# Feed-forward stages of 768 tokens: gate and up as seven quarter products, down in six groups

## What is computed

```python
D_MODEL, SEQ, CTX_LEN, DEPTH, D_FF = 1024, 512, 256, 2, 2816
def swiglu(h, w_gu, w_down):
    gate, up = jnp.split(h @ w_gu, 2, axis=-1)
    return (jax.nn.silu(gate) * up) @ w_down
for l in range(DEPTH):
    h = h + 0.5 * m[2] * swiglu(modulate(rms_norm(h, norm_ffn1[l]), m[0], m[1]), ffn1_w_gu[l], ffn1_w_down[l])
    ...   # the same for the context tokens, then the projection in, four mixers, the projection out
    h = h + 0.5 * m[8] * swiglu(modulate(rms_norm(h, norm_ffn2[l]), m[6], m[7]), ffn2_w_gu[l], ffn2_w_down[l])
```

## Time and profile before

| | |
|---|---|
| median of 3 runs | 3365.09 us (3362.91 to 3369.96) |
| the profiled execution's own time | 3367.02 us |
| its span | 3365.3 us |
| mean granted clock of TensorE | 0.985 |
| PE matmul busy | 3231.2 us, 96% |
| PE weight load busy | 2765.1 us, 82% |
| DVE busy | 1817.0 us, 54% |
| ACT busy | 1157.8 us, 34% |
| POOL busy | 439.7 us, 13% |

### The profile page before, as it was taken

One profiled execution on the slowest core, in us unless ns is written; L12 is line 12 of the kernel. 1 busy time (PEld: TensorE's weight loads), 2 busy tenths in 40 slices (PEclk: granted clock), 3 DMA queues, 4 the chain that ended last, 5 costly groups with the idle time before them and its releaser, 6 DMA issues. The chain is left out here.

```text
span 3365.3 us, 67083 instructions
## 1 busy us (share of the span) xinstructions
PE 3231.2 (96%) x28066; PEld 2765.1 (82%) x28066; DVE 1817.0 (54%) x2677; ACT 1157.8 (34%) x1839; POOL 439.7 (13%) x312
## 2 busy tenths in 40 slices
PE   6999999999988999999999999999999989899998
PEld 5888888886667878888888888888886668789897
DVE  4552554565667655543554553454555766655353
ACT  3331222225665333321222431222224654344231
POOL 2000001000705310000002000001100616120000
PEclk9999999999999999999999999999999999999999
DMA  5231221342000012222221222222232000122222
GB/s 201 91 109 66 94 96 60 127 156 89 1 17 3 4 57 81 93 98 77 90 90 57 94 98 71 81 93 85 85 141 110 2 18 3 34 88 94 90 91 94
DMA packets 68270, 263.34 MB, mean 78 GB/s; under 512 B 7552, under 2 KB 8704, under 8 KB 67456
## 3 DMA queue, kind: packets, MB, share of 16 engines
q1 hardware_dynamic: 67664, 256.95, 22.1%
q10 hardware_dynamic: 432, 3.88, 0.3%
HBM read 258.70 MB, written 2.10 MB: 77 GB/s over the span
## 5 line engine op out<-in xcount | busy, mean ns | idle before, releaser
L240 PE MATMUL ps<-hn_hi,w_hi 128*128 128x512 f32 (+1 forms) x3520 | 864.8, 327 | 17.9 <-DVE hn_lo L457 5.9
L240 PE MATMUL ps<-hn_hi,w_lo 128*128 128x512 f32 (+1 forms) x3520 | 865.4, 327 | 0.0
L240 PE MATMUL ps<-hn_lo,w_hi 128*128 128x512 f32 (+1 forms) x3520 | 861.1, 326 | 0.0
L217 ACT ACTIVATE w_hi<-raw 128x1024 fp32r<-128x1024 f32 (+1 forms) x300 | 338.5, 1128 | 1375.4 <-PE ps L240 1217.7
L222 DVE TENSOR_TENSOR w_lo<-raw,w_hi 128x1024 fp32r<-128x1024 f32 (+1 forms) x300 | 396.9, 1323 | 469.5 <-ACT w_hi L217 462.0
L240 PEld LDWEIGHTS ps<-hn_hi,w_hi 128*128 128x128 f32 x3520 | 547.9, 190 | 82.3 <-issue 17.6
L240 PEld LDWEIGHTS ps<-hn_lo,w_hi 128*128 128x128 f32 x3520 | 548.3, 190 | 58.3
L240 PEld LDWEIGHTS ps<-hn_hi,w_lo 128*128 128x128 f32 x3520 | 545.2, 190 | 58.1
L240 PE MATMUL ps<-g_hi,w_hi 128*128 128x512 f32 (+1 forms) x1424 | 398.0, 347 | 6.1 <-DVE g_lo L894 6.1
L240 PE MATMUL ps<-g_lo,w_hi 128*128 128x512 f32 (+1 forms) x1424 | 403.5, 351 | 0.0
L240 PE MATMUL ps<-g_hi,w_lo 128*128 128x512 f32 (+1 forms) x1424 | 397.5, 347 | 0.0
(11 more groups left out here) (274 smaller groups left out, 3795.8 us busy)
## 6 DMA issues: line engine op xcount, KB each, us to landing
raw<-wgu SPq DMA_DIRECT2D x176, 512.0 KB, 3.4
w_mod_one<-wmod SPq DMA_DIRECT2D x100, 512.0 KB, 3.3
raw<-wdn SPq DMA_DIRECT2D x64, 704.0 KB, 4.1
raw<-win SPq DMA_DIRECT2D x44, 512.0 KB, 4.5
w_mod_two<-wmod SPq DMA_DIRECT2D x28, 512.0 KB, 3.6
w_mod_first<-wmod_first SPq DMA_DIRECT2D x4, 2048.0 KB, 23.2
raw<-wout SPq DMA_DIRECT2D x16, 512.0 KB, 3.3
h<-xT ACTq DMA_DIRECT2D x1, 3072.0 KB, 9.8
```

The source lines that it names most:

```text
L217: act.activation(w_hi[s][:, 0:kt, :].rearrange("p k n -> p (k n)"), raw[s][:, 0:kt * P], ACT.Copy).then_inc(hi_ready[s].sem, 1)
L240: mm = pe.matmul(out[:, o:o + b - a], w[:, k, :], m[:, k, a:b], start=(k == 0 and w is w_hi[s] and m is mov_hi), stop=(k == kt - 1 and w i ...
```

## The change

For the three stages of 768 tokens `ffn` is replaced by `ffn_seven`; the last stage keeps `ffn`. The hidden tiles are taken in six groups of 4, 2, 4, 4, 4 and 4. The first group (4 pairs) is made as before, 96 matmuls to a pair. While it runs, DVE and ACT make the moving operands of the others: the normed tokens (`x_norm`) in quarters, by half of the contraction and half of the tokens, four sums of quarters, and the high and low parts of seven moving operands of 4 tiles by 386 columns.

Each of the other 18 pairs is a 2 by 2 block product (gate and up by the two halves of the contraction, times the two halves of the contraction by the two halves of the tokens) made with seven products of quarters. A quarter product has 4 contraction tiles, three products each, one span of 386 columns: 12 matmuls, 84 to a pair. DVE makes four sums of weight quarters (`weight_sum`) and the low parts; the seven results go to seven of the eight PSUM banks in turn and are put together by one ACT copy and seven DVE additions. Each weight slot has one buffer.

After each group come 8 down products over its 4 (or 2) hidden tiles, 24 (or 12) matmuls each; in the first two of them (four, in the group of 2) the last contraction tile is put off. DVE adds each to `h`, so 48 additions in a stage where there were 16. The modulation vectors stay 24 in number: two in each pair of the first group, one in pair 7, and five in the down part of each of the groups j = 2, 3 and 4. The loops are written out. The stride of `hn_hi` and `hn_lo` goes from 784 to 772 columns, and buffers are moved; the down weights are laid out in HBM in loads of 512 KB.

The diff, cut to what sets the order on each engine:

```diff
-NTP = 784
+NTP = 772
+DOWN_SIZES = (4, 2, 4, 4, 4, 4)
+            mods_of = {n: (2 * n, 2 * n + 1) for n in range(PLAIN)}
+            mods_of[FIRST[2] + 1] = (8,)
+            mods_of.update({("down", j): tuple(range(5 * j - 1, 5 * j + 4)) for j in (2, 3, 4)})
...
+            def weight_sum(eng, p, n):
+                a, b, op = {2: (quarter(2), quarter(3), ALU.add), 3: (slot_sum[2][:, :], quarter(0), ALU.subtract),
+                            4: (quarter(0), quarter(2), ALU.subtract), 5: (quarter(1), slot_sum[3][:, :], ALU.subtract)}[p]
+                slot_free(eng, p, n)
...
+                eng.tensor_tensor(slot_sum[p][:, :], a, b, op).then_inc(w_summed.sem, 1)
...
+                def _(sp):                     # loads, after a group of four pairs
+                        if z == 4:
+                            lo_there(sp, j, "01")
+                            load(0, DOWN[j, 2])
+                            lo_there(sp, j, "2")
+                            lo_there(sp, j, "3")
+                            load(1, DOWN[j, 3])
...
+                        for m in mods[:1]:
+                            load_mod(m)
+                        for s, src in enumerate(srcs):
+                            for unit in freed_by[s]:
+                                lo_there(sp, j, unit)
+                            load(s, src)
+                            for m in mods[1:] if s == 0 else ():
+                                load_mod(m)
...
+                def _(act):                    # one pair of the 18
+                            first_copy(n)
+                            if not last_of(n):
+                                gate_hi_made(n + 1)
...
+                            gate_out(n, 0)
+                            if not last_of(n):
+                                for p in (2, 3, 4):
+                                    slot_hi_made(p, n + 1)
...
+                            gate_out(n, 1)
+                            if not last_of(n):
+                                slot_hi_made(6, n + 1)
+                                slot_hi_made(5, n + 1)
+                            ring_hi_made(n, 0)
+                            ring_hi_made(n, 1)
...
+                def _(dve):
+                    def way_down(j):
...
+                        for unit in ("3", "4", "5") if z == 4 else ():
+                            down_lo_made(dve, j, unit)
...
+                        for m in mods[:1]:
+                            mod_product(m)
+                        for t in range(KD):
+                            if j < LAST and t == 7:
+                                (slot_lo_made if z == 4 else weight_sum)(dve, 5 if z == 4 else 4, n)
+                            add_down(j, t)
...
+                            if z == 4 and t == 1:
+                                down_lo_made(dve, j, "6")
+                            if j < LAST and t == (2 if z == 4 else 0):
+                                gate_lo_made(n)
+                            for m in mods[1 + t:2 + t]:
+                                mod_product(m)
...
+                            if z == 4 and t == 3:
+                                down_lo_made(dve, j, "7")
...
+                            if j == LAST and t:
+                                gained_lo(dve, t - 1, nxt[3], hn_hi_ready.at(KD + 1 + t + 1), nxt[4])
...
+                            gate_first(n)
+                            if not last_of(n):
+                                gate_lo_made(n + 1)
+                                weight_sum(dve, 2, n + 1)
...
+                            with_sixth(n)
+                            with_fifth(n)
+                            if not last_of(n):
+                                weight_sum(dve, 3, n + 1)
+                                slot_lo_made(dve, 2, n + 1)
...
+                            with_seventh(n)
+                            if not last_of(n):
+                                weight_sum(dve, 4, n + 1)
...
+                            gate_second(n)
+                            if not last_of(n):
+                                weight_sum(dve, 5, n + 1)
+                                slot_lo_made(dve, 3, n + 1)
+                                slot_lo_made(dve, 4, n + 1)
...
+                            up_first(n)
+                            if not last_of(n):
+                                slot_lo_made(dve, 6, n + 1)
+                            silu(n, 0)
+                            silu(n, 1)
+                            glu_out(n, 0)
+                            glu_out(n, 1)
+                            if not last_of(n):
+                                slot_lo_made(dve, 5, n + 1)
+                            ring_lo_made(n, 0)
+                            ring_lo_made(n, 1)
+                        way_down(j)
...
+                def _(pe):
+                        for o, p in enumerate(order_of(n)):
+                            if p < 2:
+                                lo_there(pe, "gate", n)
+                            else:
+                                lo_there(pe, p, n)
+                            i = 7 * q + o
+                            if i < 8:
+                                t = 4 + i // 2
+                                pe.wait_ge(evacuated[t % 2].sem, evacuated[t % 2].at(KD // 2 * (j - 1) + t // 2 + 1))
...
+                            for k in range(LP):
...
+                                for w, m in ((slot_hi[p], M_OF[p][0]), (slot_hi[p], M_OF[p][1]), (slot_lo[p], M_OF[p][0])):
+                                    mm = pe.matmul(bank(n, p), w[:, k, :], m[:, k, 0:HW],
...
+                        together = 2 if z == 4 else 4
+                        for t in range(together):
+                            down(j, t, range(z - 1))
+                        for t in range(together):
+                            down(j, t, (z - 1,))
+                        for t in range(together, KD):
+                            down(j, t, range(z))
```

More of the change, by code:

```diff
@@ L79, in build_trunk @@
         R_G = R_N + 2 * KD * NTP * 4
-        R_W = R_G + 2 * NFH * NT * 4
-        R_T = R_W + 6 * NFH * P * 4
+        WS = KD * P * 4 + 1568
+        R_T = R_G + 2 * NFH * NT * 4 + 6 * NFH * P * 4 + 768
+        R_W = R_T - 6 * WS
+        assert R_W >= R_G + 2 * NFH * NT * 4
         arena_size = nc.sbuf_usable_end - start
@@ L109, in build_trunk @@
         lnv = at("lnv", [P, NT], R_G + 3 * TOK)
-        WS = NFH * P * 4
         raw = [at(f"raw{s}", [P, NFH * P], R_W + s * WS) for s in range(2)]
@@ L566, in load_down @@
                             for s in range(2):
-                                load_block(sp, s, A["wdn"][l, which, half, i * 2 + s], NFH, i + (b0 + NFH))
+                                load_block(sp, s, A["wdn_last"][half, i * 2 + s], NFH, i + (b0 + NFH))
                         load_down(0)
@@ L741, in ffn @@
                 mod_end((sum(MODS),), 2)
+        LP = KD // 2
+        MS = 386
+        SLOT = LP * P * 4
+        MBLOCK = 2 * LP * MS * 4
+        SIZES = DOWN_SIZES
+        FIRST = [sum(SIZES[:j]) for j in range(len(SIZES))]
+        GROUP_OF = [j for j, z in enumerate(SIZES) for _ in range(z)]
+        BLOCK_OF = (0, 1, 6, 4, 2, 3, 5)
+        M_OF = [(at(f"m_hi{p}", [P, LP, MS], R_N + i * MBLOCK, F32R),
+                 at(f"m_lo{p}", [P, LP, MS], R_N + i * MBLOCK + MBLOCK // 2, F32R)) for p, i in enumerate(BLOCK_OF)]
@@ new lines, in build_trunk @@
+        t1_raw = at("t1_raw", [P, LP, MS], R_N + BLOCK_OF[2] * MBLOCK + MBLOCK // 2)
+        R_X = R_N + 7 * MBLOCK
+        x_norm = at("x_norm", [P, 2, KD, 386], R_X)
+        ring_first = [at(f"ring_first{i}", [P, 4, NT], R_N + 4 * MBLOCK + i * 4 * NT * 4, F32R) for i in range(2)]
+        ring_next = [at(f"ring{i}", [P, 4, NT], R_X + i * 4 * NT * 4, F32R) for i in range(2)]
+        assert 2 * KD * NTP * 4 <= 4 * MBLOCK and 4 * MBLOCK + 8 * NT * 4 <= 6 * MBLOCK
+        R_S = R_X + 2 * KD * 386 * 4
@@ new lines, in build_trunk @@
+        assert R_S + 3 * SLOT <= R_W
+        S_HI = [R_W + 2 * WS, R_W + 2 * WS + SLOT, R_S, R_S + SLOT] + [R_W + 4 * WS + 2 * SLOT + i * SLOT for i in range(3)]
+        S_LO = [R_W + 4 * WS, R_W + 4 * WS + SLOT] + [R_W + 2 * WS + (2 + i) * SLOT for i in range(2)]
+        S_LO += [R_S + 2 * SLOT, R_W + 2 * WS + 4 * SLOT, T0]
+        pair_hi = {0: w_hi[0], **{p: at(f"pair_hi{p}", [P, KD, P], S_HI[p], F32R) for p in (2, 4)}}
+        pair_lo = {0: w_lo[0], 2: at("pair_lo2", [P, KD, P], S_LO[2], F32R)}
@@ new lines, in build_trunk @@
+        slot_hi = [pair_hi[p // 2 * 2][:, p % 2 * LP:(p % 2 + 1) * LP, :] for p in range(6)]
+        slot_hi.append(at("slot_hi6", [P, LP, P], S_HI[6], F32R)[:, :, :])
+        slot_lo = [pair_lo[p // 2 * 2][:, p % 2 * LP:(p % 2 + 1) * LP, :] for p in range(4)]
+        slot_lo += [at(f"slot_lo{p}", [P, LP, P], S_LO[p], F32R)[:, :, :] for p in (4, 5, 6)]
+        slot_sum = {p: at(f"slot_sum{p}", [P, LP * P], S_LO[p]) for p in range(2, 6)}
+        gate_s = at("gate_s", [P, 2 * 386], T0 + SLOT)
```

(27 more changed lines are left out.)

594 lines of the change are left out of this document (added).

## The result

The changed kernel takes 3385.75 us (median of 4 runs, 3385.62 to 3386.97) against 3364.8 us before: a ratio of 1.006, 95% interval 1.0047 to 1.0072. It is slower by 21 us where 96 us less were forecast.

The account below looks back on a forecast made before the run. PE, busy 96% of the span, was taken as the bound: 3367.0 - 125.8 (pairs) + 21 (down-part stalls) + 4.8 (group 0) + 3.4 (stage ends) = 3270.4, or 3269 us against the median; range 3238 to 3305 us.

Parts of the forecast that it names:

- the upper end: New pairs on PE: 177.1 ns a matmul at 386 columns instead of the 174.2 taken; gain 112 us, not 125.8.
- DVE's work in a pair: New pairs: DVE needs 13.6 us of PE's 14.63; 15.9 us if nothing overlaps.
- only behind it stands the addition of tile 4: Down parts, groups 2 to 4: fifth vector ends D + 35.0, tile 4's addition D + 36.2; stall 2.3 us, nine times, 21 us.
- D: The time when PE begins a down part; times in that part are counted from it.
- The chain of vectors itself: Down parts, groups 2 to 4: five vectors from one buffer, first load landing at D + 10.2, then 5.64 us a vector.
- a falling clock: Sign of being wrong: the granted clock falls in a stage; no size was given.
- the end of the stage: Block end: tile 6's low part stands behind DVE's last addition, 1.14 us more, three times, 3.4 us.
- It ends before DVE: Stage end: POOL's square and sum, 3.8 us a tile, stay under the new 4.24 us and end before DVE.
- group 0: Two vectors in the fourth plain pair delay the up product's scaling: PE waits 1.6 us, three times, 4.8 us.
- The one that ended slower: Rival, down parts: landings stretch to 5.4 us each; at 6.0 a stall is 15.8 us, total 3387 us; chance 0.04.
- DVE as the bound: Rival, pairs: at 15.9 us a pair DVE falls behind, costing 31 us, total 3300 us; chance 0.13.
- only the columns are saved: Rival, pairs: each loses only 1.89 us, gain 102 us, total 3293 us; chance 0.05.

Follow-up runs that it names:

- run 3: Changed kernel with POOL squaring only residual tile 0 in the last down part of the three changed stages: 3365.7 us, 0.9998 of the kernel before.
- run 4: Changed kernel plus 96 matmuls each at 386, 384, 258, 322, 450 and 512 columns behind the last store: 3471.98 us, one execution.
- run 1: Changed kernel with only the low part of down tile 7 made ahead of the fifth modulation vector: 3339.39 us, 0.992 of the kernel before.
- run 8: Changed kernel, tile 7's low part earlier, vector 7 in first down part, one of each five vectors in the last pair, its successor's load earlier: 3280.84 us, 0.9739.

## Why the prediction was wrong

**The account.** 113 us less for the pairs. Against it, from the two lists of waits: 63.8 us at tile 7, 12.8 in the first down part, 25.6 - 5.1 = 20.5 at the blocks and some 3 for additions and ring parts, together 100 us. That leaves 13 us less, and the kernel is 21 us slower. The 34 us between are the clock behind the 15 gaps: the windows have 34 us there, and the kernel before has no stretch at the lower level in the corresponding part of any stage. The runs bear it out: filling nine gaps gave 18 us (19.2 by the windows), and moving vector 7 gave 21, of which 12.8 + 2.0 are waits and 6 are left (6.7 by the windows). The three block ends were not filled by themselves; their 7.8 us stand on the windows and on run 3.

The 117 us above the forecast of 3269 us are, but for 1 us of rounding: 13 for the pitch, 43 more of waits behind the vectors in the down parts (63.8 for 21), 17 at the blocks, 8 in the first down parts, 3 for small waits, and 34 for the clock.

**What held.** PE is the bound and doesn't wait inside a pair. The pair came out at the upper end (14.87; 14.88 there, 14.63 taken), which is 13 us of the miss: the pitch was mis-sized, 177.0 ns for 174.2, and an even stream has 175.4 (run 4). DVE's work in a pair was put at 13.6 us and is 13.5. The groups' hand-over of the hidden tile cost under 1 us in all.

**The step that failed, first:** "only behind it stands the addition of tile 4". The order of DVE's program was misread. In the loop over t the vector stands ahead of the low part of tile 7, so what waits behind the fifth vector is not only the next group's bank, wanted at D + 33.9, but tile 7's weights, wanted at D + 29.7. The chain of vectors itself was right in kind: the first came at D + 9.7 (373.13 - 363.46; 10.2 was said) and the distance was 6.05 us (5.64), of which 0.3 are the load's (3.6 us to landing for 3.3). With the order that I had read, run 1 has 2.7 us a group where 2.3 were forecast.

**Second, a term that the sum lacked:** the clock. Every gap was priced at its own length. The gaps of 7.1, 4.3 and 8.5 us cost 2.1, 2.2 and 2.6 us each on top. The prediction had named a falling clock as a sign of being wrong, and gave it no price.

**Third, the end of the stage:** 1.1 us were forecast, 6.8 measured (8.5 - 1.7). "It ends before DVE" looked at when POOL is done, not at what it does to DVE. With POOL at work two low-part instructions take 3.9 us, without it 1.13 (run 3); before, they could be slow at no cost, in a gap of 11.7 us a tile, and the new tile has 4.24. The Trainium skill, "SBUF — State Buffer", section "SBUF: two separate sides", says that a VectorE instruction with two SBUF inputs and a GpSimd instruction that reads SBUF exclude each other for a whole instruction. The trace agrees in direction (3.89 against 1.13 us, and no change for the additions that read PSUM), and it was the rule to look for.

**Fourth, group 0:** 4.3 us a stage, 1.6 forecast. DVE scaled the gate product 2 us late, since the vector of the pair before was still in work (its second instruction starts at 106.98, the scaling at 108.12), and the distance to the next vector was 5.9 us.

**The rivals.** The one that ended slower named the right place, the chain of vectors, and the wrong cause: it needed landings of 5.4 us, and they are 3.6. That the time came out near its 3387 (its own terms give 3390) is luck: the waits and the clock that make it up are others. DVE as the bound fell, and that only the columns are saved would have left a pair at 15.07.

## What to carry to other kernels

When an engine's slack is a few us, write down its program in the order of the code, one line for each instruction, before pricing it: one subtraction behind a wait for a load cost 46 us here. A vector that waits for its own load doesn't fill slack, it blocks DVE's queue; start the load earlier and spread the vectors, as run 8 did. Look in the old trace for an instruction that is longer beside another engine's work: it costs nothing in a slack of 11.7 us and shows in one of 4.24. And price a gap of several us on TensorE with what the clock takes behind it.

## What the runs showed that was not expected

A PE gap of 7.3 us is followed by work at half clock (0.51 in 400 to 405), 2.3 us of loss; over all nine it is 2.1 us a gap. Dummy matmuls in the gap win that back, 18 us in nine gaps. Two DVE instructions with two SBUF inputs go from 1.13 to 3.89 us beside POOL's square and sum, and to 2.8 beside the sum alone. And a wait that the profile gives to "issue" can be an engine's: the three of 4.4 us were DVE's scaling, which ended 0.1 us before PE started.
